# A one-core fp32 model kernel: three pairs of unused SBUF columns between its buffers change their widths

## The reference

```python
for layer in range(DEPTH):                      # DEPTH = 2
    x = x + 0.5 * swiglu(rmsnorm(x, ffn1_norm[layer]), ffn1_w_in[layer], ffn1_w_out[layer])
    h = rmsnorm(x, mix_norm[layer])
    x = x + (attn_lru_mixer, deltanet_mixer)[layer](h, ...)
    x = x + cross_attention(rmsnorm(x, xa_norm[layer]), rmsnorm(mem, ...), wq, wkv, wo)
    x = x + 0.5 * swiglu(rmsnorm(x, ffn2_norm[layer]), ...)
x = rmsnorm(x, final_norm)
for i in range(4):                              # second block
    y = (retention, conformer_conv, gla)[i % 3](rmsnorm_2(h, gains[i, 0]), ...)
    h = h + rmsnorm_2(y, gains[i, 1])
    h = h + rmsnorm_2(square(relu(rmsnorm_2(h, gains[i, 2]) @ w_up)) @ w_down, gains[i, 3])
```

## Time and profile before

| | us |
|---|---|
| median of 3 runs | 2697.3 (2697.28 to 2699.07) |
| the profiled execution's own time | 2697.3 |
| its span, first to last instruction | 2695.5 |
| PE busy | 2616.5 (97%) |
| PEld busy | 2531.0 (94%) |
| DVE busy | 1816.9 (67%) |
| ACT busy | 1408.2 (52%) |
| DMA queue of the weights, share of 16 engines | 49.9% |

### The profile page before, as it was taken

How to read it: one execution, slowest core, us unless ns; L and a number is a source line. 1 busy time by engine, 2 the same in 40 slices (tenths; PEclk the granted TensorE clock), 3 DMA queues, 4 the chain that set the end, 5 groups by cost and what they waited for, 6 DMA issues and landing times. The chain is left out here.

```text
span 2695.5 us, 49224 instructions
## 1 busy us (share of the span) xinstructions
PE 2616.5 (97%) x21088; PEld 2531.0 (94%) x21088; DVE 1816.9 (67%) x2374; ACT 1408.2 (52%) x1935; POOL 0.2 (0%) x4
## 2 busy tenths in 40 slices
PE   8999999999998899999999999989999999999998
PEld 8999999999987889999999999979988999989998
DVE  6658766666657646766756866878564786756774
ACT  6446655454457255544446566454455545446553
POOL 0000000000000000000000000000000000000000
PEclk9999999999999999999999999999999999999999
DMA  6554545556543234555544555225643555544553
GB/s 249 179 192 162 173 146 201 193 192 195 193 137 106 81 123 149 194 194 188 182 155 159 179 195 180 79 104 190 194 158 102 175 193 192 178 167 146 178 194 133
DMA packets 129866, 450.12 MB, mean 167 GB/s; under 512 B 20209, under 2 KB 21105, under 8 KB 129521
## 3 DMA queue, kind: packets, MB, share of 16 engines
q1 hardware_dynamic: 129504, 446.83, 49.9%
q10 hardware_dynamic: 144, 0.14, 0.0%
HBM read 445.48 MB, written 1.44 MB: 166 GB/s over the span
## 5 line engine op out<-in xcount | busy, mean ns | idle before, releaser
L274 PE MATMUL B<-R,WH 128*128 128x256 f32 x10432 | 2028.9, 280 | 19.5 <-DVE R L1226 8.6
L274 PEld LDWEIGHTS B<-R,WH 128*128 128x128 f32 x10432 | 1659.6, 189 | 32.6 <-issue 10.1
L1011 DVE TENSOR_TENSOR WL<-SL,WH 128x1024 fp32r<-128x1024 f32 x835 | 1006.5, 1223 | 668.2 <-ACT WH L2091 666.7
L274 PE MATMUL B<-R,WL 128*128 128x256 f32 x4480 | 1244.3, 278 | 0.0
L2091 ACT ACTIVATE WH<-SL 128x1024 fp32r<-128x1024 f32 x835 | 862.3, 1053 | 463.8 <-PE B L274 448.4
L274 PEld LDWEIGHTS B<-R,WL 128*128 128x128 f32 x4480 | 846.9, 189 | 0.0
L274 PE MATMUL B<-RB,WH 128*128 128x256 f32 x1984 | 548.9, 277 | 0.3 <-DVE WL L1011 0.3
L274 PE MATMUL B<-RB,WL 128*128 128x256 f32 x1728 | 477.9, 277 | 0.0
L274 PEld LDWEIGHTS B<-RB,WH 128*128 128x128 f32 x1984 | 372.7, 188 | 0.6 <-DVE WL L1011 0.5
L274 PEld LDWEIGHTS B<-RB,WL 128*128 128x128 f32 x1728 | 324.6, 188 | 0.0
L274 PE MATMUL B<-WH,R 128*128 128x512 f32 x480 | 157.1, 399 | 0.0
(11 more groups left out here) (293 smaller groups left out, 1570.3 us busy)
## 6 DMA issues: line engine op xcount, KB each, us to landing
SL<-in_w SPq DMA_DIRECT2D x835, 512.0 KB, 3.3
CP<-in_cp SPq DMA_DIRECT2D x5, 768.0 KB, 5.1
PG<-in_mem SPq DMA_DIRECT2D x1, 1024.0 KB, 13.0
PK<-in_pk SPq DMA_DIRECT2D x1, 594.5 KB, 9.0
XG<-in_xT SPq DMA_DIRECT2D x1, 512.0 KB, 7.4
out<-XG SPq DMA_DIRECT2D x1, 512.0 KB, 2.6
SL<-in_w SPq DMA_DIRECT2D x1, 384.0 KB, 3.5
XG<-in_xT SPq DMA_DIRECT2D x1, 256.0 KB, 5.8
```

The costliest lines, as they stand in the source:

```text
L274: return p.matmul(o, left, right, start=first, stop=final, skip_group_check=True)
L1011: v.tensor_tensor(WL[t % NRAW][:, :], SL[t % NRAW][:, :], WH[t % NSPL][:, :].bitcast(F32), ALU.subtract).then_inc(s_lo, 1)
```

## The change

Four numbers change, all widths of columns that nothing uses. ROOM0 goes from 112 to 16 columns (of 4 bytes), ROOM and ROOM1 together from 80 to 48, ROOM2 from 96 to 32.

```diff
@@ -134,14 +134,14 @@
         XG = sb("XG", 2064)
         X = XG[:, 16:2064]
         H = sb("H", 2048)
-        sb("ROOM0", 112)
+        sb("ROOM0", 16)
         with ExitStack() as names:
             WL = [names.enter_context(nc.sbuf_tensor(f"WL{i}", [128, 1024], F32R)) for i in range(NRAW)]
-            names.enter_context(nc.sbuf_tensor("ROOM", [128, 80], F32))
+            names.enter_context(nc.sbuf_tensor("ROOM", [128, 48], F32))
             RB, R03, R45, R67 = (names.enter_context(nc.sbuf_tensor(n, [128, c], F32R))
                                  for n, c in (("RB", 8192), ("R03", 8192), ("R45", 4096), ("R67", 4096)))
         SL = [sb(f"SL{i}", 1024) for i in range(NRAW)]
-        sb("ROOM1", 80)
+        sb("ROOM1", 48)
         BIG = sb("BIG", 8192)
         PG = [sb(f"PG{i}", 2048) for i in range(12)]
@@ -152,7 +152,7 @@
         PK = sb("PK", NPK)
-        sb("ROOM2", 96)
+        sb("ROOM2", 32)
         WH = [sb(f"WH{i}", 1024, F32R) for i in range(NSPL)]
```

## The result

The changed kernel takes 2735.0 us, the median of 4 runs (2723.94 to 2738.24), against 2697.29 for the kernel before (4 runs, 2696.85 to 2699.07): ratio 1.0132, 95% interval [1.0101, 1.0162]. So it is slower, where no change was forecast, and its runs spread over 14 us where those of before spread over 2. Its profiled execution took 2722.2 us, 2720.4 of them span, 24.9 more than before.

A forecast was written before the change was run, and what follows sets the result against it. TensorE was taken as the bound, 18,624 fp32r matmuls at 113.3 ns filling 2110 of 2695.5 us. Four terms of 0 on the profiled 2697.3 us gave a forecast of 2697.3 us, range 2676 to 2719.

The forecast's parts named there:

- Term 1: Spacing of the 18,624 fp32r matmuls of 256 columns: stays at 113.3 ns, 0 us; outer bounds -102 and +88 us.
- The nearest row is the main form itself at its two distances, which says 0.: Main fp32r matmuls: WH and WL, at two distances from the rows, both show 277 ns, so 0 was taken.
- A stream that nobody's address disturbs.: Main matmul stream: PE keeps 355, 356 and 355 matmuls per 40 us however busy DVE and ACT are.
- The agreement of the fp32 products at several distances: Fp32 products: 379 ns at distances 0 and 256, 215.6 against 216.4 ns at others, taken as support for 0.
- The slower rival: Main matmuls: weight load meets moving rows at distance 320; 1.1 ns each gives 2718 us, 4.7 ns 2785; chance 0.18.
- one shared place for the weights: Main matmuls: low and high weights, formerly at two places in 512 bytes, now share 256, so each may start later.
- 320 as a new distance: Main matmuls: weights come 320 bytes past the moving rows, a distance no fp32r row of this form holds.
- The faster rival: Main matmuls: a clash of moving rows and weight load lessens at 320 bytes; 1.1 ns each, 2677 us; chance 0.22.
- Terms 2, 3 and 4: Wide matmuls, weight conversions and tile loads: 0 us each; ends 1.6 either way, 0 to +2, and -5 to +5.
- term 2: The 720 matmuls of 512 columns, weights moving: 0 us taken, at most 1.6 us either way.

The follow-up runs named there:

- e6: Kernel before with only ROOM2 96 to 128, moving WH to the low weights' place, 192 bytes past the moving rows; 2759.9 us, ratio 1.0227.
- e8: Kernel before with ROOM0 128, ROOM and ROOM1 64: SL and WL move up by 64 bytes, WH stays; 2764.5 us, ratio 1.0249.
- e14: Changed kernel, all buffers kept, with only TensorE's reads of the low stationary weights displaced by 128 bytes; 2696.4 us, ratio 0.9994 to the kernel before.
- e15: Kernel before, all buffers kept, with only TensorE's reads of the low stationary weights displaced by 128 bytes; 2724.7 us, ratio 1.0103.
- e5: Kernel before with ROOM0 16, ROOM and ROOM1 176, ROOM2 128, putting low weights at 64 and high at 192 modulo 256; 2757.1 us, ratio 1.0215.
- e11: Kernel before with ROOM0 96, ROOM and ROOM1 96: SL and WL move from 192 to 128 bytes past the rows; 2769.7 us, ratio 1.0265.
- e3: Kernel before with ROOM0 16, ROOM and ROOM1 176: only SL and WL move, by 384 bytes; 2724.0 us, ratio 1.0108.
- e10: Kernel before with only ROOM2 96 to 80: WH moves from 64 to 0 bytes past the rows; 2759.2 us, ratio 1.0227.
- e12: Kernel before with ROOM and ROOM1 80 to 72, ROOM2 96 to 104: activation rows alone move 32 bytes down; 2763.1 us, ratio 1.0243.
- e4: Kernel before with ROOM0 16, ROOM and ROOM1 176, ROOM2 32: WL and WH move as in the change, activations stay; 2729.1 us, ratio 1.0118.
- e9: Changed kernel with 12 extra fp32 products of 256 columns in the MLP product stages; 2732.5 us, ratio 1.0122 to the kernel before.
- e1: Kernel before with only ROOM0 112 to 16: weights, activations and WH move down together by 384 bytes; 2697.5 us, ratio 1.0001.
- e2: Kernel before with only ROOM2 96 to 32: WH alone moves, from 64 to 320 bytes past the rows; 2697.1 us, ratio 1.0000.
- e13: Kernel before with 12 extra fp32 products of 256 columns in the MLP product stages; 2703.5 us, ratio 1.0020.
- e7: Kernel before with ROOM0 80, ROOM and ROOM1 112: SL and WL move from 192 to 64 bytes past the rows; 2721.9 us, ratio 1.0085.

## Why the prediction was wrong

**Term 1 failed, and alone made the result.** It took 0 where 1.76 ns a matmul were measured in the profiled run, 32.1 us: some 7,400 matmuls more than before at a spacing 4.5 ns wider. The medians are 37.7 us apart, but no run near the median has a trace. Three steps in it went wrong.

- "The nearest row is the main form itself at its two distances, which says 0." WH at 64 and WL at 192 show the same spacing because they alternate in one stream of TensorE. The stream has one rhythm at a time, and which ones it can have depends on the pair. Two members of it are not two samples of a dependence on distance. e6 and e8 move one member and slow the loads of both.
- "A stream that nobody's address disturbs." show that DVE and ACT don't disturb it, and e14 and e15 confirm this. The step from there to TensorE's own second read was not covered by any row.
- The agreement of the fp32 products at several distances carried nothing over to fp32r, as the prediction half admitted. They stay at 216 ns in every kernel here.

**The slower rival was right in place, and had a low chance, 0.18.** It named the weight load and the moving rows, and the runs show that their places relative to each other decide. Its 1.1 ns and 2718 us compare with 1.76 ns and 2722 us in the profiled run and 2735 us in the median, between the 0.3 ns from which it decides and its outer 4.7. It had every matmul a little later; measured were 44% of them later by 4.5 ns and the others not at all. Its price of 4.7 ns came from 118 ns in the earlier trace rows, which I read as a disturbance by the fp32 products beside it. By size it was the second spacing, 4.5 ns above the first. Those rows asked for a question that was not put: why does it take several matmuls to recover, and would it always? Its picture of one shared place for the weights was wrong in part, as e5 shows, and so was 320 as a new distance: modulo 256 it is 64.

**The faster rival** was wrong. None of the 16 pairs is under 113.3, so none of the 5.5 ns over 107.8 was to be had by placing in steps of 64 bytes. What they are stays open. The Trainium skill's gap of N / 2.4 + 2.5 ns ("TensorE: Matmul & The Clock Gate", section "Back-to-back issue gap"), which it calls the gap of an isolated matmul, is 109.2 here; no stretch or stage measured here reaches it. The same page says, in "Step-by-step: what each phase is for", that TensorE has two independent read ports and that loading the next weights takes no read bandwidth from the running matmul. e14 and e15 don't fit that: where the load reads changes the spacing of the running stream by 4%. By what path is not shown.

**Terms 2, 3 and 4 held.** The wide matmuls are 229.9 ns apart against 230.4 (-0.4 us over 720 of them), line 1011 has 1222 ns, line 2091 has 1052, waits for loads are 8.8 us. The bound on term 2 was too narrow for other places, since these matmuls are 233.3 ns apart in e6 and e8. The stretch that was to show term 1 has 1230 matmuls in the changed kernel, against 1238:

```profile
2540.00:2680.00 140.00, 139.58 (x1230) 139.36 (x1229) 98.72 (x115) 68.56 (x82) 0.00 (x0) 1.00 0.58 192
```

That looks like +0.7 ns a matmul and is none: the program comes later, and a break near 2551 us falls into the stretch. The matmuls themselves are at 113.3 there, as 355 from 2620 to 2660 show. One stretch can't judge a kernel whose stages differ; the counts of several can.

## What to carry to other kernels

Where a stream of fp32r matmuls bounds a kernel, the addresses of the stationary operands relative to the moving one, modulo 256 bytes, are a tuning parameter worth up to 2.7% here (e11 against the kernel before), and every edit that shifts a buffer changes it unasked. Read the spacing in several long stretches, and treat a wider spread between runs (14 us against 2 in the first runs; 30 us in e3 and 20 in e5, which have two spacings, but 3 to 6 in e6, e8, e10, e11 and e12, which are slow throughout) and two values of the spacing in one trace as a sign of it. A few matmuls in a row at a wider spacing, even where they recover, can be a rhythm that another layout keeps.

## What the runs showed of the hardware

- Equal matmul streams have two stable spacings, 113.3 and 117.8 ns for 256 columns at a granted clock of 1.00, in kernels at place (64, 64), and 113.3 and 118.9 ns in e5. With few exceptions each lasts from one break to the next, for up to 1582 matmuls (e4); a break is another kind of product or a pause. The same program takes 14 us (the changed kernel) to 30 us (e3) more or less from run to run, so it seems not to fix which; each kernel has one trace, and this was not seen in two traces of one kernel.
- Each of e9's 12 extra products switched the spacing to the other one.
- At place (192, 64) only the faster one lasts: in e1, e2, e13 and e14 the other ends within 8 to 10 matmuls. At (0, 64) and (192, 192) nearly only the slower one does.
- The dependence repeats every 256 bytes, as far as e2 and e7 show. It is of the places of TensorE's own reads (e14, e15), and in the stretches counted here DVE's and ACT's work beside them changes neither spacing. What inside TensorE or its memory paths meets was not found, nor what sets the spacing at a start.
